# A hybrid decoder layer on eight cores: the recurrence of its time-mixing half, hopped through precomputed chunk matrices

## The reference, cut to what matters

```
state = state * w_t + (state @ a_t) b_t^T + v_t k_t^T
y_t   = state @ r_t
```

## Time and profile before

| | |
|---|---|
| median of the three runs shown | 3254.41 us (3156.46, 3254.41, 3404.91) |
| the profiled execution | 3152.11 us; span of its slowest core 3149.6 us |
| spans of the eight cores | 3074.3 to 3149.6 us |
| busy in the span: TensorE, VectorE, ScalarE, POOL | 78%, 44%, 40%, 7% |
| mixer, 200 to 1450 us | TensorE busy 1054 of 1250 us, granted clock 0.87 |
| sixteen tiles, 1785 to 2452 us | TensorE busy 562 of 667 us, granted clock 0.95 |

### The profile page before, as it was taken

How to read it: one execution, slowest core, us unless ns; L and a number is a source line. 1 busy time by engine, 2 the same in 40 slices (tenths; PEclk the granted TensorE clock), 3 DMA queues, 4 the chain that set the end, 5 groups by cost and what they waited for, 6 DMA issues and landing times.

```text
span 3149.6 us, 53016 instructions; the slowest of 8 cores (3074.3 to 3149.6 us)
## 1 busy us (share of the span) xinstructions
PE 2461.8 (78%) x23096; PEld 1283.7 (41%) x23096; DVE 1391.5 (44%) x2657; ACT 1254.0 (40%) x2399; POOL 225.3 (7%) x374
## 2 busy tenths in 40 slices
PE   1698688787888888887575288888888697979796
PEld 1344344343444444444452144444444354545453
DVE  4455455465656566665112023233232344444544
ACT  3665455455655565555111022222222233242422
POOL 1000000000000100000100000000000001010101
PEclk6799788898988988886688699999999798989898
DMA  9256766636353544242675988665622556656562
GB/s 198 91 76 82 88 87 78 96 61 113 72 108 69 109 81 101 60 95 95 141 252 147 143 152 165 136 140 128 147 81 80 191 186 213 213 193 223 169 226 72
DMA packets 106735, 406.21 MB, mean 129 GB/s; under 512 B 26208, under 2 KB 52320, under 8 KB 91520
## 3 DMA queue, kind: packets, MB, share of 16 engines
q0 software_dynamic: 30656, 195.54, 35.3%
q1 hardware_dynamic: 75840, 207.21, 20.4%
HBM read 530.96 MB, written 184.68 MB: 227 GB/s over the span
## 4 chain that ended last, share of the span: by engine, by line
PE 68%; DVE 11%; ACT 9%; DMA 8%; another core or an unknown queue 2%; issue 2%; POOL 0%; SPq 0%; POOLq 0%
PE ps L128 68%; ACT big L144 9%; DVE big L151 5%; DVE big L156 4%; DMA mixd<-big 2%; DMA big<-kvc 2%; DMA big<-x 2%; DVE big L172 1%; DMA big<-h_s,big 1%; DMA out<-big 1%; DVE big L165 1%; DMA big<-woc 1%; DMA big<-wqc 0%; DMA h_s<-big 0%
## 5 line engine op out<-in xcount | busy, mean ns | idle before, releaser
L128 PE MATMUL ps<-big 64*64 64x64 bf16 (+8 forms) x23096 | 2461.8, 278 | 661.4 <-ACT big L144 234.4
L128 PEld LDWEIGHTS ps<-big 64*64 64x64 bf16 (+3 forms) x23096 | 1283.7, 111 | 1839.1 <-ACT big L144 390.3
L144 ACT ACTIVATE big<-big 128x512 f32<-128x512 f32 (+7 forms) x926 | 602.6, 672 | 930.7 <-DVE big L151 470.7
L151 DVE TENSOR_TENSOR big<-ps,big 128x512 bf16<-128x512 f32 (+4 forms) x616 | 435.8, 723 | 749.4 <-PE ps L128 685.4
L144 ACT ACTIVATE big<-ps 128x512 bf16<-128x512 f32 (+3 forms) x940 | 432.2, 484 | 571.3 <-PE ps L128 569.9
L144 ACT ACTIVATE big<-ps,big 128x512 f32<-128x512 f32 (+4 forms) x364 | 227.4, 631 | 369.0 <-PE ps L128 316.7
L172 DVE CAST big<-ps 128x64 bf16<-128x64 f32 (+1 forms) x364 | 130.3, 359 | 386.7 <-PE ps L128 385.2
L156 DVE SCALAR_TENSOR_TENSOR big<-ps,big 128x512 f32<-128x512 f32 (+1 forms) x316 | 227.0, 722 | 142.9 <-ACT big L144 101.7
L156 DVE SCALAR_TENSOR_TENSOR big<-big 128x512 f32<-128x512 f32 (+4 forms) x206 | 213.5, 1042 | 50.7 <-ACT big L144 47.5
L151 DVE TENSOR_TENSOR big<-big 128x512 bf16<-128x512 f32 (+12 forms) x406 | 203.5, 512 | 69.9 <-ACT big L144 64.2
L156 DVE SCALAR_TENSOR_TENSOR big<-big,ps 128x64 f32<-128x64 f32 x280 | 92.3, 330 | 93.1 <-PE ps L128 90.2
(11 more groups left out here) (25 smaller groups left out, 154.1 us busy)
## 6 DMA issues: line engine op xcount, KB each, us to landing
big<-x SPq DMA_DIRECT2D x32, 1024.0 KB, 7.4
wgc<-wg_l POOLq DMA_DIRECT2D x64, 512.0 KB, 12.2
wuc<-wu_l POOLq DMA_DIRECT2D x64, 512.0 KB, 15.7
wdc<-wd_l POOLq DMA_DIRECT2D x64, 512.0 KB, 23.6
big<-wgc SPq DMA_DIRECT2D x64, 512.0 KB, 4.4
big<-wuc SPq DMA_DIRECT2D x64, 512.0 KB, 4.6
big<-wdc SPq DMA_DIRECT2D x64, 512.0 KB, 4.6
kvc<-w_kv POOLq DMA_DIRECT2D x32, 512.0 KB, 19.1
```

The lines of the kernel that those rows point to most:

```text
L128: r.append(e.matmul(out, lhsT=lhsT, rhs=rhs, start=st, stop=sp_, **k))
L144: return self.op("act", lambda e: e.activation(out=out, in_=in_, func=func, **kw), dur, R, W, P, tbl=TBL.get(func))
L151: return self.op(eng, lambda e: e.tensor_tensor(out=out, in0=a, in1=b, op=op), dur, R, W, P)
```

## The change

`st_chain` loses two of its four steps. `st_solve` now applies the inverse beforehand, for all eight chunks at once: it makes K times V and a transposed copy of A with two more groups of 16 matmuls in `s1`, then TT times both (32 matmuls in `pair`), then their products with TB and with NB (32 matmuls in `pair`), which are stored over A and R (in AR). Five ScalarE copies and one VectorE addition carry these out, written in place over halves of KB, NB and AR. A chunk of the chain is then one group of six matmuls into Z (two TB, two TK, and last two with the old state), VectorE's `stt`, ScalarE's cast, and six matmuls into Y.

Z no longer has its own bank. For chunks 0 to 6 it is summed in the output bank `bky`, in the columns that the next chunk's Y will overwrite; for the last chunk it takes a bank of `pr`. Since the recorded reads and writes are by bank, Y of a chunk now waits for the `stt` that reads Z. The freed bank goes to `pr` (four banks), `TTr` shrinks to one buffer and `mixr` grows to three.

The 160 recasts of the mixer are tied to the Y matmuls of single chunks, one in one or two chunks, from unit 0 to unit 28. The 96 later ones are tied to single VectorE additions of the tiles (eight per tile), so that each waits for the addition before it may go.

```diff
-        TVr, TBr, TKr, TTr = [m.bf16s(2, QT) for _ in range(4)]
+        TVr, TBr, TKr = [m.bf16s(2, QT) for _ in range(3)]
+        TTr = m.bf16s(1, QT)
...
-        Xb, Ub, Zr, Sb = m.bf16s(2, 64), m.bf16s(2, 64), m.f32s(2, 64), m.bf16s(2, 64)
+        Zr, Sb = m.f32s(2, 64), m.bf16s(4, 64)
...
-        mixr = m.bf16s(2, QT)
+        mixr = m.bf16s(3, QT)
...
-        pr = Ring(bank[3:6])
-        bkc, bky = bank[6].fresh(), bank[7].fresh()
+        pr = Ring(bank[3:7])
+        bky = bank[7].fresh()
...
 # st_solve, after the first squaring
+            V_3, K3, T3 = r3(tr[0].a, 8), r3(KB.a, 8), None
+            S.mm(quad(lambda h, c: Q8[HS[h], c, :], lambda h, c: K3[HS[h], c, 0:64], lambda h, c: V_3[HS[h], c, :], 64), R=[KB, tr[0]], W=[s1])
+            S.act(K3[:, :, 0:64], Q8, AF.Copy, R=[s1], P=[KB])
+            S.mm(quad(lambda h, c: Q8[HS[h], c, :], lambda h, c: A3[HS[h], c, 0:64], lambda h, c: i64b.a[HS[h], :], 64), R=[AR, i64b], W=[s1])
+            S.act(NB3[:, :, 0:64], Q8, AF.Copy, R=[s1], P=[NB])
...
 # st_solve, at its end
+            S.mm(quad(lambda h, c: P8[HS[h], c, 0:64], lambda h, c: T3[HS[h], c, :], lambda h, c: NB3[HS[h], c, 0:64], 64) +
+                 quad(lambda h, c: P8[HS[h], c, 64:128], lambda h, c: T3[HS[h], c, :], lambda h, c: K3[HS[h], c, 0:64], 64), R=[TT, NB, KB], W=[pair])
+            S.act(NB3[:, :, 0:64], P8[:, :, 0:64], AF.Copy, R=[pair], P=[NB])
+            S.act(K3[:, :, 0:64], P8[:, :, 64:128], AF.Copy, R=[pair], P=[KB])
+            S.mm(quad(lambda h, c: P8[HS[h], c, 0:64], lambda h, c: NB3[HS[h], c, 0:64], lambda h, c: TB3[HS[h], c, :], 64) +
+                 quad(lambda h, c: P8[HS[h], c, 64:128], lambda h, c: NB3[HS[h], c, 0:64], lambda h, c: NB3[HS[h], c, 64:128], 64), R=[NB, tr[1]], W=[pair])
+            S.act(A3[:, :, 0:64], P8[:, :, 0:64], AF.Copy, R=[pair], P=[AR])
+            S.tt(A3[:, :, 64:128], P8[:, :, 64:128], A3[:, :, 64:128], ALU.add, R=[pair, AR], P=[AR])
...
 # st_chain, per chunk
-                S.mm(it, R=[KB, TV, AR] + ([Sp] if Sp else []), W=[bkc])
-                X = Xb.next()
-                S.act(X.a, cxa, AF.Copy, R=[bkc], W=[X])
-                S.mm([(cua[HS[h], :], T3[HS[h], c, :], X.a[HS[h], :], True, True) for h in range(2)], R=[TT, X], W=[bkc])
-                Uu = Ub.next()
-                S.cp(Uu.a, cua, R=[bkc], W=[Uu])
-                S.mm([(cza[HS[h], :], C3[HS[h], c, :], V3[HS[h], c, :], True, False) for h in range(2)] +
-                     [(cza[HS[h], :], B3[HS[h], c, :], Uu.a[HS[h], :], False, True) for h in range(2)], R=[TK, TV, TB, Uu], W=[bkc])
+                bkc = bky if c < 7 else pr.next()
+                cza = bkc.a[:, 64 * (c + 1) % 512:64 * (c + 1) % 512 + 64]
+                it = [(cza[HS[h], :], B3[HS[h], c, :], K3[HS[h], c, 0:64], True, False) for h in range(2)]
+                it += [(cza[HS[h], :], C3[HS[h], c, :], V3[HS[h], c, :], False, Sp is None) for h in range(2)]
                 if Sp is not None:
...
+                    it += [(cza[HS[h], :], A3[HS[h], c, 0:64], Sp.a[HS[h], :], False, True) for h in range(2)]
+                S.mm(it, R=[KB, TV, TB, TK, AR] + ([Sp] if Sp else []), P=[bkc])
...
-                    it.append((y, Uu.a[HS[h], :], N3[HS[h], c, 64:128], Sp is None, False))
+                    it.append((y, K3[HS[h], c, 0:64], N3[HS[h], c, 64:128], Sp is None, False))
...
-                S.mm(it, R=[AR, NB, KB, TV, Uu] + ([Sp] if Sp else []), P=[bky])
+                S.mm(it, R=[AR, NB, KB, TV] + ([Sp] if Sp else []), P=[bky])
+                marks.append(S.ops[-1])
...
 # recasts
-        free_u = [u for u in range(1, 31) if u % 4 != 3]
...
-            S.dma("pool", d_, s_, P=[bs], after=[marks[free_u[ji * len(free_u) // len(jobs)]]])
+            S.dma("pool", d_, s_, P=[bs], after=[marks[ji * 232 // len(jobs)]])
...
+            def recast(o):
+                nj[0] += 1
+                while (nj[1] - len(ejobs)) * 120 < nj[0] * nj[1] and ejobs:
+                    d_, s_, bs = ejobs.pop(0)
+                    S.dma("pool", d_, s_, P=[bs], after=[o])
...
-                for d_, s_, bs in ejobs[len(ejobs) * tt // 16:len(ejobs) * (tt + 1) // 16]:
-                    S.dma("pool", d_, s_, P=[bs], R=[mxb])
...
                     S.tt(hb[:, ds_], b.a, hb[:, ds_], ALU.add, R=[b, hq[db]], W=[hq[db]])
+                    recast(S.ops[-1])
```

More of the change, by code:

```diff
@@ L678, in st_proj @@
                 U["rkv"[t]] = z
-            marks.append(S.ops[-1])
         def st_prep(u):
@@ L768, in st_solve @@
                     S.tt(r3(TT.a, 8), P8[:, :, 64:128], W3[:, :, 64:128], ALU.add, R=[pair, W0], W=[TT])
-            U.update(NB=NB, KB=KB, TV=tr[0], TB=tr[1], TK=tr[2], TT=TT)
-        cxa, cua, cza = [bkc.a[:, i * 64:(i + 1) * 64] for i in range(3)]
+            T3, TB3 = r3(TT.a, 8), r3(tr[1].a, 8)
+            S.mm(quad(lambda h, c: P8[HS[h], c, 0:64], lambda h, c: T3[HS[h], c, :], lambda h, c: NB3[HS[h], c, 0:64], 64) +
[6 more added lines that the diff above has]
+            S.tt(A3[:, :, 64:128], P8[:, :, 64:128], A3[:, :, 64:128], ALU.add, R=[pair, AR], P=[AR])
+            U.update(NB=NB, KB=KB, TV=tr[0], TB=tr[1], TK=tr[2])
         chain = dict(S=None, Z=None, G=None)
@@ L775, in st_chain @@
             U = units[u]
-            A3, N3, K3, V3, B3, C3, T3 = [r3(U[n].a, 8) for n in ("AR", "NB", "KB", "TV", "TB", "TK", "TT")]
-            AR, NB, KB, TV, TB, TK, TT, GL = [U[n] for n in ("AR", "NB", "KB", "TV", "TB", "TK", "TT", "GL")]
+            A3, N3, K3, V3, B3, C3 = [r3(U[n].a, 8) for n in ("AR", "NB", "KB", "TV", "TB", "TK")]
+            AR, NB, KB, TV, TB, TK, GL = [U[n] for n in ("AR", "NB", "KB", "TV", "TB", "TK", "GL")]
             Y3 = r3(bky.a, 8)
@@ L783, in st_chain @@
                 Sp = chain["S"]
-                it = []
-                for h in range(2):
-                    it.append((cxa[HS[h], :], K3[HS[h], c, 0:64], V3[HS[h], c, :], True, Sp is None))
+                bkc = bky if c < 7 else pr.next()
+                cza = bkc.a[:, 64 * (c + 1) % 512:64 * (c + 1) % 512 + 64]
+                it = [(cza[HS[h], :], B3[HS[h], c, :], K3[HS[h], c, 0:64], True, False) for h in range(2)]
+                it += [(cza[HS[h], :], C3[HS[h], c, :], V3[HS[h], c, :], False, Sp is None) for h in range(2)]
                 if Sp is not None:
-                    for h in range(2):
-                        it.append((cxa[HS[h], :], A3[HS[h], c, 0:64], Sp.a[HS[h], :], False, True))
-                S.mm(it, R=[KB, TV, AR] + ([Sp] if Sp else []), W=[bkc])
-                X = Xb.next()
-                S.act(X.a, cxa, AF.Copy, R=[bkc], W=[X])
-                S.mm([(cua[HS[h], :], T3[HS[h], c, :], X.a[HS[h], :], True, True) for h in range(2)], R=[TT, X], W=[bkc])
-                Uu = Ub.next()
-                S.cp(Uu.a, cua, R=[bkc], W=[Uu])
-                S.mm([(cza[HS[h], :], C3[HS[h], c, :], V3[HS[h], c, :], True, False) for h in range(2)] +
-                     [(cza[HS[h], :], B3[HS[h], c, :], Uu.a[HS[h], :], False, True) for h in range(2)], R=[TK, TV, TB, Uu], W=[bkc])
+                    it += [(cza[HS[h], :], A3[HS[h], c, 0:64], Sp.a[HS[h], :], False, True) for h in range(2)]
+                S.mm(it, R=[KB, TV, TB, TK, AR] + ([Sp] if Sp else []), P=[bkc])
                 Z = Zr.next()
@@ L1051, in routing @@
                          R=[ohr, Fr], P=[tabp])
+            nj = [0, len(ejobs)]
+            def recast(o):
[3 more added lines that the diff above has]
+                    S.dma("pool", d_, s_, P=[bs], after=[o])
             for tt in range(NTT):
```

## The result

The changed kernel ran in 2856.81 us in its profiled execution, where the kernel before took 3152.11. The medians, 2923.02 us of four runs and 3212.32 of four, mix in executions in which one die ran slower; without those the ratio is **0.904**, 95% interval 0.894 to 0.914. In a later series of six the profiled execution was 2858.24 us and the ratio 0.9043 again, 0.901 to 0.908. So the change is worth 295 us in the profiled executions, of 188 that were forecast. The sign was right and the range held the time, 7 us above its lower end; a third of the gain was not foreseen, and this part asks where it came from.

A forecast was written before the change was run, and what follows sets the result against it. No engine is full; in the mixer TensorE is close and waits for short steps of others. 3152 - 96 (idle time) - 30 (clock) - 10 (last unit) - 52 (start of tiles) = 2964 us; range 2850 to 3075 us.

The forecast's parts named there:

- Start of the tiles, 52 us: First tile's `mixd` load, held behind twelve recasts, would land in 9.7 to 11.3 us instead of 62.5: 52 us gone.
- The bare chunk and the tail: Last unit's chain: a chunk falls from 2.30 to 1.1 to 1.2 us, saving 10 us over eight chunks.
- Stores to `mixd`, 45 us: Mixer: stores late behind seven recasts hold a `mixr` buffer ScalarE waits for; spacing and third buffer save 45 us (0 to 64).
- TensorE's idle time, 96 us less: Mixer: idle time falls from 196 to 100 us, by 26 (copy of U), 15 (copy of X), 10 (rest), 45 (stores).
- the rest (norms, preparation, the state's own two hops): Mixer's other waits: a denser order and fourth `pr` bank may give something or nothing; taken as 10 us.
- 26 + 15 + 10 = 51 us: Mixer idle time saved: 26 us copy of U, 15 us copy of X, 10 us other stages.
- The clock, 30 us: Mixer's granted clock rises from 0.87 towards 0.95: a third of 89 us taken, 30 us; ends 0 and 89.
- The solve's matmuls, 0 us: Mixer: 64 more 64x64 matmuls per unit cancel against fewer stretches of 64-row work: 0 us, ends -38 to +54.
- The first: Mixer: Y's wait for `stt` in the shared bank replaces the hops, 82 us new idle time, 3046 us; chance 0.17.
- The second: Denser than taken: mixer idle time falls to 50 us, clock reaches the tiles' level, 2855 us; chance 0.13.
- The third: Recasts did not hold the loads; hole and stores stay, only copy of U and tail come, 3116 us; chance 0.11.
- The fourth: Mixer: the solve becomes the bound through single-buffered `pair` and `s1`, 198 us added, 3243 us, slower; chance 0.07.

The follow-up runs named there:

- this part alone: Kernel before with only the tiles' 96 recasts tied one by one to additions, without the burst; 3091.67 us.

## Why the prediction was right, and where it was too small

**Start of the tiles, 52 us: right.** 49 in the change, 54 with this part alone.

**The bare chunk and the tail: right.** 1.13 us where 1.1 to 1.2 were worked out; 8 x (2.30 - 1.13) = 9.4 us for a term of 10.

**Stores to `mixd`, 45 us: the number held, the reason only in the old mixer.** There the part is worth 47 us, 28 of them idle time. In the new mixer the same spacing is worth 58 or 59 us, and 30 to 38 of these are instructions that arrive late.

**TensorE's idle time, 96 us less: close in sum (113), wrong in its terms, and so by luck.** The step that failed is the one on the rest (norms, preparation, the state's own two hops): "I take 10". The hops were to give up 26 + 15 + 10 = 51 us of waits for ScalarE and VectorE; with the recurrence alone, bursts and two `mixr` buffers as before, 151 us went (206 to 56), and 162 with the whole change. (Part of the 151 may be the stores, for which ScalarE waited 19 us there and not 49.7.) The prediction read each wait as the property of the instruction that ended it. With two hops in place of four the other stages' results are there when their turn comes: before full-width bf16 matmuls idle time fell from 62.3 to 4.3 us. That it is the hops and not the new order of the queues that does this is argued; no run has the one without the other. Against it stood 50 us of new issue waits, which no term and no rival named, and the two errors cancel.

**The clock, 30 us: the term that was too small.** The step was "short operations don't scale in full, so I take a third" of 89. TensorE's busy time in the mixer fell by 123 us with 2059 more matmuls. If all of the 1105 us followed the granted clock from 0.86 to 0.95, that would be 105 us (an estimate from the two windows). The prediction's own upper end was the better reading.

**The solve's matmuls, 0 us: right, beside the clock.** 64x64 work fell by 37 us, and 33 of that is what the clock's ratio gives; 2048 more matmuls cost nothing on top. A 64x64 matmul now takes 305.8 / 11744 = 26 ns of busy time, where it took 343.1 / 9696 = 35, or 32 at the new clock by ratio. The recurrence alone has this too: 26 ns at a clock of 0.93.

**The rivals.** The first fell: TensorE's waits for L156 went from 21.5 to 9.8 us, where the rival asked for 82 us more. The rule of the Trainium skill (PSUM — Partial Sum Buffer, summary of rules), to read one bank while matmuls write another, has no price in these rows: the run that follows it is 23 us slower in the mixer, with one bank less for `pr`. The second, with a chance of 0.13 against 0.52 for the forecast, named the time (2855 us) and its clock, though not its idle time: 108 us remained where it had 50. The third fell with the tiles' recasts alone: the burst held the load, though the two queues take turns, 192 packets against 192, since the burst's packets are of 32 KB and the load's of 512 B. The round-robin rule of the Trainium skill (DMA: Bandwidth & Descriptors, section SWDGE vs HWDGE vs iDMA), from which the prediction drew this rival, agrees with these rows; that the row of 62.5 us speaks against it was a wrong reading, since turns by packets don't get small packets past large ones. The fourth fell: the kernel is not slower, and TensorE, busy for 90% of the mixer, is the bound.

Of the 236 us that the mixer gave, 136 were forecast. The 100 us missed are 93 us of busy time (123, of which 30 were forecast) and 7 us of idle time (113, of which 106 were forecast, the tail with it).

## What to carry to other kernels

When a change takes hops out of a serial chain that runs between other work on a nearly full engine, count the waits of all stages that share its buffers, and let TensorE's whole busy time follow the clock: here 51 us of waits named became 151, and 30 us of clock became about 105. Once that engine is dense, look at its "issue" row and at what DMA traffic runs beside it; fewer transfers in the dense stretch (160 to 64) were worth 75 us there, though part of it is paid where they go. A burst of transfers tied to one event is worth spacing, and a run with that part alone settles it. Look at packet sizes too: where queues take turns by packets, a load in small packets beside large ones gets little through.

## What the runs showed of the hardware

- TensorE's instructions come by DMA in blocks of 256, and large DRAM-to-DRAM transfers beside dense 64x64 matmuls make them late: 60.5 us in 24 waits of up to 7.4 us with 160 transfers of 1 MB read and 0.5 MB written in the mixer, 98.9 us in 37 when they come in bursts, 8.6 us with 64, 2.0 us with none. Cutting the transfers' 32 KB packets into 4 KB ones left 58.4 us.
- Two DMA queues took turns by packets, 192 to 192 and 1590 to 1588 in 30 us, so the bytes went with the packets' sizes: a load of 1 MB in 512 B packets took 62.5 us beside 32 KB packets.
- The mixer's granted clock was 0.86 with TensorE idle for 17% of it, 0.93 at 13%, 0.95 at 10%, 0.98 at 6 and 5%; but the kernel with two `s1` buffers had 0.95 at 15%, so the idle share alone does not set it.
- A sum that is read from the PSUM bank of another result (Z in `bky`) left waits of at most 9.8 us for its reader in a mixer of 1090 us.
